# A trunk step on one core: 224 dense tokens for 240 in the expert layer, 32 gathered prompt tokens on four copies, and eight places for halves of the V table

## What is computed

```python
q = (hf @ wq).reshape(t, 8, 2, 128)
s1 = einsum('thd,nd->thn', q[:, :, 0], k1)          # 128 keys
s2 = einsum('thd,nd->thn', q[:, :, 1], k2)
v1, i1 = top_k(s1, 16); v2, i2 = top_k(s2, 16)
cs, ci = top_k(all 256 sums v1 + v2, 16)
e = i1[ci // 16] * 128 + i2[ci % 16]                 # one of 16384 experts
g = softmax(cs)
act = gelu(einsum('tkd,td->tk', u_tab[e], h))        # 8 heads x 16 experts a token
out = einsum('tk,tkd->td', g * act, v_tab[e])
```

## Time and profile before

| | |
|---|---|
| median of three runs | 4571.98 us |
| the profiled execution | 4579.46 us |
| its span, first to last instruction | 4577.7 us |
| PE busy | 4429.2 us, 97% |
| PEld busy | 3699.4 us, 81% |
| DVE busy | 2653.2 us, 58% |
| ACT busy | 556.3 us, 12% |
| POOL busy | 1000.1 us, 22% |
| mean granted TensorE clock | 0.983 of full speed |
| DMA | 1387.06 MB, 303 GB/s over the span |

### The profile page before, as it was taken

One profiled execution on the slowest core, in us unless ns is written; L12 is line 12 of the kernel. 1 busy time (PEld: TensorE's weight loads), 2 busy tenths in 40 slices (PEclk: granted clock), 3 DMA queues, 4 the chain that ended last, 5 costly groups with the idle time before them and its releaser, 6 DMA issues.

```text
span 4577.7 us, 50690 instructions
## 1 busy us (share of the span) xinstructions
PE 4429.2 (97%) x20466; PEld 3699.4 (81%) x20466; DVE 2653.2 (58%) x4333; ACT 556.3 (12%) x1399; POOL 1000.1 (22%) x755
## 2 busy tenths in 40 slices
PE   8999999999999999899999899998899998999998
PEld 7888888888767576567776679998799987889988
DVE  4434500016688787766665558887667755555552
ACT  1111100001111111110000010001334300000000
POOL 1000000000112223024443233233322322222220
PEclk9999999999999999999999999999899999999999
DMA  4444444455489779679999789999999999999995
GB/s 169 136 143 143 168 147 155 161 191 179 176 285 361 288 274 382 230 289 407 387 394 388 295 340 380 389 391 366 367 381 383 388 370 393 366 410 420 423 422 180
DMA packets 269932, 1387.06 MB, mean 303 GB/s; under 512 B 46977, under 2 KB 53377, under 8 KB 141586
## 3 DMA queue, kind: packets, MB, share of 16 engines
q0 software_dynamic: 99600, 720.05, 39.5%
q1 hardware_dynamic: 170098, 663.77, 39.4%
HBM read 1341.95 MB, written 40.29 MB: 302 GB/s over the span
## 4 chain that ended last, share of the span: by engine, by line
PE 65%; DMA 18%; DVE 12%; issue 4%; POOL 1%; ACT 0%; POOLq 0%; DVEq 0%; SPq 0%; ACTq 0%
PE ps L417 33%; PE ps L772 9%; DMA RING<-in_peer_u,table 7%; PE pm L792 7%; PE ps L792 7%; DMA RA<-in_peer_v 6%; DMA RING<-in_peer_v,table 4%; DVE BIG L1296 3%; PE ps L659 2%; PE ps L592 2%; DVE RING L1005 2%; DVE CUR L1013 2%; PE ps L783 1%; DMA BIG<-in_peer_v,table 1%; PE pm L480 1%
## 5 line engine op out<-in xcount | busy, mean ns | idle before, releaser
L417 PE MATMUL ps<-X,BIG 128*128 128x320 f32 (+1 forms) x5632 | 1412.3, 413 | 16.3 <-DVE BIG L1201 12.1
L417 PEld LDWEIGHTS ps<-X,BIG 128*128 128x128 f32 x5632 | 1080.3, 193 | 331.4 <-issue 22.0
L1013 DVE SCALAR_TENSOR_TENSOR CUR<-RING,wexp,CUR 128x2048 f32<-128x2048 f32 x304 | 714.5, 2350 | 305.8 <-DMA RING<-in_peer_v,table 163.4
L772 PE MATMUL ps<-X,RA 128*128 128x240 f32 x4096 | 846.8, 368 | 16.1 <-ACT BIG L1990 14.2
L1005 DVE CUSTOM_DVE_ANT_0 RING<-RING,CUR 128x2048 f32<-128x2048 f32 x286 | 653.3, 2291 | 338.9 <-DMA RING<-in_peer_u,table 219.0
L772 PEld LDWEIGHTS ps<-X,RA 128*128 128x128 f32 x4096 | 777.1, 191 | 69.3 <-ACT BIG L1990 14.9
L2123 POOL DMA_INDIRECT RING<-in_peer_v,table x224 | 337.9, 1508 | 823.9 <-DVE CUR L1013 664.7
L417 PE MATMUL ps<-BIG 128*128 128x256 f32 (+1 forms) x2048 | 506.3, 409 | 11.6 <-DVE BIG L1484 9.3
L2123 POOL DMA_INDIRECT RING<-in_peer_u,table x222 | 335.0, 1509 | 780.8 <-DVE hidden L1005 507.9
L417 PEld LDWEIGHTS ps<-BIG 128*128 128x128 f32 x2048 | 391.8, 192 | 121.5 <-DVE BIG L1484 10.8
L792 PE MATMUL ps<-BIG,RA 128*128 128x240 f32 x2048 | 443.5, 371 | 22.7 <-DMA RA<-in_peer_v 22.2
(11 more groups left out here) (322 smaller groups left out, 2976.0 us busy)
## 6 DMA issues: line engine op xcount, KB each, us to landing
BIG<-in_w_in_b SPq DMA_DIRECT2D x128, 1024.0 KB, 5.6
RA<-in_uT SPq DMA_DIRECT2D x256, 512.0 KB, 7.8
RA<-in_peer_v SPq DMA_DIRECT2D x256, 512.0 KB, 9.2
BIG<-in_w_gb_b SPq DMA_DIRECT2D x32, 1024.0 KB, 5.4
BIG<-in_w_ga_b SPq DMA_DIRECT2D x32, 1024.0 KB, 5.2
BIG<-in_w_gla_o_b SPq DMA_DIRECT2D x32, 1024.0 KB, 6.6
BIG<-in_w_mix_b SPq DMA_DIRECT2D x32, 1024.0 KB, 6.6
BIG<-in_w_q_b SPq DMA_DIRECT2D x32, 1024.0 KB, 6.9
```

Of the source, the lines that this page charges most:

```text
L417: last = pe.matmul(bank[:, 0:n], w(k, j * P, P), src[:, k, 0:n], start=(k == 0), stop=(k == kt - 1))
L772: last = pe.matmul(bank[:, 0:ND], half_slot[slot_of[m]][:, k % 8, :], h2T[1][:, k, 0:ND], start=(k == 0), stop=(k == KT - 1))
L1013: row_used.on(dve.scalar_tensor_tensor(out=cur[0:n, :], in0=row, scalar=wexp[0:n, par, k:k + 1], in1=cur[0:n, :], op0=ALU.mult, op1=ALU.ad ...
```

## The change

Five edits.

1. ND goes from 240 to 224. All that follows from it changes with it: 32 prompt tokens are gathered in tile 3, on four copies with two heads each (64 rows and two merges in place of 32 and three), the one-hot groups are 56 and begin at block 71 in place of 67, `H` has 224 columns a block. There are 707 rows.
2. V's halves get four more places, in the part of `BIG` that held the first blocks of `H`, which are free once V's product has read them (`h_over`). The last 16 halves use the four old places.
3. In the second group's heads the place "conv" has 9.6 for 12.0, and four taps in place of five have a row ahead of them.
4. Group 1's routing begins in its queries: 10.0 behind each head's spare work from head 2 on.
5. In the first part of U's stage routing is paced with 2.7 for 3.4, and rows with 3.8 for 3.9 until all routing but the softmax is done, and 4.1 then.

```diff
-ND = 240
+ND = 224
+V_MORE = 4
-        vhalf = [part_of(RA, 1024 * i, 1024) for i in range(4)]
+        vhalf = [part_of(RA, 1024 * i, 1024) for i in range(4)] + [part_of(BIG, 1024 * i, 1024) for i in range(V_MORE)]
-        last_in, loads = {}, [0] * 4
+        last_in, loads = {}, [0] * (4 + V_MORE)
+
+        def h_over(i):
+            return (1024 * (i - 3) - 1) // ND
+
         for m in range(4 * NB):
-            s = min(range(4), key=lambda i: last_in.get(i, i - 4))
+            b = (m - 2 * NB) // 2
+            free = [i for i in range(4 + V_MORE) if i < 4 or i in last_in or b >= h_over(i) + 3]
+            if m >= 4 * NB - 16:
+                free = range(4)
+            s = min(free, key=lambda i: last_in.get(i, i - 8))
...
-                    if g and tap in (3, 7, 11, 15, 25):
+                    if g and tap in (3, 9, 15, 25):
                         run(work, 2.4)
...
                 if g:
-                    spare((h, "conv"), 12.0)
+                    spare((h, "conv"), 9.6)
...
                     spare((g, hd, "wq"), (16.0, 12.0)[g])
+                    if g and hd >= 2:
+                        run(work_1, 10.0)
...
                 if b < G_AT - 1:
-                    paced(work_1, 3.4)
-                    paced(work, 3.9)
+                    paced(work_1, 2.7)
+                    paced(work, U_PACE if routed.n == ROUTED else 3.8)
...
+                elif s >= 4:
+                    sp.wait_ge(*v_half.at(h_over(s), 1))
```

More of the change, by code:

```diff
@@ L342, in trunk @@
         x_loaded = [signal(f"x_loaded{i}") for i in range(4)]
-        uv_loaded = [signal(f"uv_loaded{i}") for i in range(4)]
+        uv_loaded = [signal(f"uv_loaded{i}") for i in range(4 + V_MORE)]
         g_copied = signal("g_copied")
```

## The result

| | before | changed |
|---|---|---|
| median | 4573.56 us (8 runs, 4562.12 to 4597.51) | 4612.44 us (8 runs, 4606.13 to 4618.32) |
| ratio, with its 95% interval | 1 | 1.0081 [1.0065, 1.0097] |
| span of the profiled execution | 4577.7 us | 4615.3 us |
| TensorE busy | 4429.2 us | 4315.9 us |
| moved by DMA | 1387.06 MB | 1420.62 MB |

The changed kernel is 0.8% slower, 39 us. TensorE has 113.3 us less work (the difference of its busy times) and the DMA engines 33.6 MB more. The lines of the program have moved: L417, L772, L783 and L792 are now L426, L781, L792 and L801, the row lines L1005 and L1013 are L1014 and L1022, the merge L1009 is L1018, the last norm L806 is L815, and L1576 is L1587.

What follows compares the result with a forecast made beforehand. The gather, DMA-bound, ends last: last row 4479.9 - 16 + 18.6 + 80 - 4 + 12 = 4570.5, then the tail to span 4616; with 1.8 around it and 7.5 less for the median, 4610 us; range 4530 to 4680.

Steps and rivals of the forecast that it cites:

- a long wait for the one-hots: Sign of being right: in U's front TensorE waits long for VectorE's one-hots, since U's front gains nothing.
- Tile 1's start: Gather's first row of tile 1: root asked one query place later, +18.6 us, less 16 from the heads; about 2648.
- The heads: Second group's heads: fewer rows before the gated value cut TensorE's waits, 16 us taken, bounds 0 and 34.
- Routing is VectorE work, and the gather in U waits for DMA, so I give it 0: U's stage: six pairs of routing remain instead of ten, the rest moved to the queries; no gain counted.
- 32.5 MB more: From tile 1's first row on: 33 rows added, one query weight of 2.1 MB ahead instead; 80 us.
- 388 to 423 GB/s for it: DMA rate for the added bytes along the gather: 84 us at 388, 77 at 423; 80 taken.
- Rival B: V's stage runs at its late rate, 423 GB/s, throughout: 48 us less, 4562; chance 0.16.
- The rows alone, +12 us: After TensorE finishes V, last 150 us: 0.25 us added for each of 50 rows; bounds 0 and 85.
- My mark, more than 3.6 us a row: Row spacing at the end: less than 2.8 us or more than 3.6 decides between A and C.
- rival C: Rows alone at the end are slot-bound: three places, 9.0 us landing, 4.2 us a row; 4683; chance 0.15.
- Eight places: V's stage: eight places for halves remove TensorE's 22.2 us of waits but add no bandwidth; off the gather's path.
- The tail: Behind the last row: 13.8 us to the tile's output, about 10 for sums, then 17.7 plus 4 for low clock.

Runs made afterwards that it cites:

- the fourth place: The changed kernel with a fourth place again for gathered rows from row 570 on: 4573.95 us, 38 us faster than the changed kernel.
- the last run: The kernel before with seven rows fewer in the heads, eight places for V's halves and a fourth gathered-row place from row 570: 4550.41 us, 0.9925.

## Why the forecast was right, and which terms were off

The forecast was 4610 us and 4612.44 came. The mechanism, the gather ends last and TensorE's 113 us are hidden behind it, is shown by the runs with 32 rows fewer (-116 us) and with V's product halved (-16 us here, -48 in the kernel before). Part of the closeness is luck: terms were off by 20 us and more, in both directions.

- **What was right.** TensorE lost 113.3 us of work; half products follow each other at 3.03 us, 189 ns an instruction, so the weight loads don't hold them at 191. The waits for V's halves nearly vanish, VectorE doesn't wait for TensorE's tiles, U's front gains nothing, and TensorE's last half product but one ends 129 us before the last row (150 said).
- **One sign that failed.** I had said a long wait for the one-hots. TensorE waits 12.4 us there (L792), and 39.9 us for ScalarE's gelu (L781) ahead of it, which the forecast didn't have.
- **Tile 1's start**, 2648 said, 2644.1 found. The heads gave 20 us (U starts at 2727.03 for 2747.26), 4 more than I took, and the root's later place took them back. I had charged that place to the routing in the queries. The runs show that it belongs to the heads: with the heads' edit alone U starts 25.5 us earlier and the root is there only 7.0 earlier (2628.29 for 2635.32), 18.5 less, which is one query place, and with the routing alone it stays at 2635.49.
- **"Routing is VectorE work, and the gather in U waits for DMA, so I give it 0".** Wrong. Rows 256 to 288 take 153 us for 135. The reason that I see, argued and not tried apart: there are three or four places for rows, and what VectorE doesn't read isn't fetched anew. Edits 4 and 5 alone cost 12 to 19 us, and 9 of the 12 in the span are there at the first one-hot, behind the late gelu; in the sum of the changed kernel this was made up by the higher rates below.
- **32.5 MB more.** The rows are 32 more and not 33: VectorE reads 704 for 672, beside three merges for four, and the DMA total grows by 33.6 MB and not 34.6. Yet between tile 1's first row and the last, the windows give 1936 x 0.389 = 753 MB for 1835 x 0.388 = 712: 41 MB more. I had counted the rows, and left out the table blocks that lay behind 4480 before and now lie ahead of the last row, though I named them a few lines later. I put them at 11 blocks, 11.5 MB; the windows show 8.6 MB more than the 32.5 in the sum, 22 us.
- **388 to 423 GB/s for it.** I took a full DMA for granted, and 388 was too low in U's back and at the start of V. Same stretches in the kernel before, and then in the changed kernel (us, PE busy, clock, share, GB/s):

```profile
3250.00:3600.00 350.00, 350.00 (x1901) 1.00 0.98 385
3700.00:4050.00 350.00, 325.19 (x1539) 0.99 1.00 385
```

```profile
3250.00:3600.00 350.00, 350.00 (x2016) 1.00 1.00 406
3700.00:4050.00 350.00, 327.94 (x1677) 1.00 1.02 410
```

A share of 0.98 or 1.00 had looked full at 385 GB/s, and 21 to 25 more went through. In U's back TensorE is busy for all 350 us in both kernels, and does 2016 instructions for 1901, 6.0% more, while the rate rises by 5.5%: there it was TensorE that set the pace of the table, and not the DMA. Over these 350 us each that is worth 350 x 21/385 = 19 us in U's back and 23 in V; from 4050 to 4440 the changed kernel is slower (412 for 421), 8 us. The rest, some 34 us, pays for the term before this one and a part of the next. Rival B's rate did come, in part.
- **The rows alone, +12 us.** The mis-sized term. I gave a lone row 0.25 us over 2.5; it took 3.6 to 3.7 (116 us in the medians and 118.3 in the traces for the 32 rows left out). From 4450 to 4579 the 37.6 MB take 129 us, and at 407 GB/s they would take 93: 36 us, near the middle of the bounds 0 and 85. My mark, more than 3.6 us a row, spoke for rival C, and C's mechanism is shown by the fourth place. Its price was too high, because alone a row lands in 7.5 us and not in the 9.0 that its 4.2 us were worked out from: with 7.5 the same working, (7.5 + 2.35 + 1.3)/3, gives the 3.7 measured. It was also put on top of a middle that ran faster than I had it. So my forecast named the right end and had C's mechanism inside its last stretch.
- **Eight places** I gave nothing. They cost 7 us here by the medians, not clear of the intervals of the ratios: halves come early, TensorE ends V at 4450 instead of 4519, and more rows are left to run alone.
- **The tail** is 36.7 us from the last row's end to the end of the span, for 45.5 said: 12.4 for 13.8 to the tile's output, 7.5 for 10 to the sums behind the last half product (4598.48), and 16.8 for 21.7 from there, where the 4 us for the low clock didn't come.

In all the last row came 8 us later than said (4 earlier at tile 1's start, 12 later in the middle: 99.9 us for 88), and the tail gave 9 back.

The Trainium skill's ceiling of 435 GB/s ("DMA: Bandwidth & Descriptors", Where 436 GB/s comes from) agrees with the runs here: the best window of 340 us is 424 GB/s, in the last run. The same section says of transfers between HBM and SBUF that a core's share of HBM, about 358 GB/s, binds first; these loads are of that kind and went at 385 to 424, so for this case the measurement decides. The 435 is a bound, and the 129 us at 292 GB/s show what it leaves out: whether enough is in flight.

## What to carry to other kernels

Where two streams share a DMA that is nearly full and different engines end them, a place given to one took from the other in these runs: the same four places gave 37 us, or cost 7, and the same fourth row place gave 38 us, or cost 23 (by the medians), depending on which stream ended last. Look first at which ends last and by how much, give places until the two end together, and take an edit that moves work to the fuller resource only once that is done. When a stream is left alone at the end, its rate is that of its own places in flight, so read its landing time there, and not its share beside others.

## What the runs showed of the hardware

- Three indirect gathers of 1 MiB in flight, alone, move 292 GB/s at a share of 0.80 (129 us), with 7.5 us from issue to landing; four move 395 at 0.98 (14 us), with a landing of 6.9 to 7.8.
- Doubling the half-megabyte loads in flight lifted their landing from 9.3 to 17 us. A fourth row place moved the split between the two streams more than the total: 8 places for halves beside 4 for rows stretched a half's landing to 26.0 us, 8 beside 3 had 11.6, at 424 and 419 GB/s. The number of places alone doesn't give the landing: 8 beside 3 is 17 us in the changed kernel, at 409.
- A share of 1.00 stood at 385 GB/s in one stretch, and 1.02 at 421 in the next, of the same kernel (3700 to 4050, and 4050 to 4440, before); in the changed kernel it was 410 at 1.02 and 412 at 1.01. With four places again in the changed kernel it was 395 and 411. So the mean busy share doesn't tell how much more goes through. What lowers the rate ahead of 4050 wasn't tried, and stays open.
